# Where split operands begin in SBUF: four weight slots at offsets of 16 bytes, the rest on multiples of 128

## The chip, the cores and the metric

The kernel runs on one core of one Trainium2 chip. The metric is the device time of one execution in microseconds; the kernel before takes 3706.04 us (median of 3 runs, 3702.63 to 3710.48).

## What is computed

The reference is a trunk of two layers over 512 frames of width 1024, in float32. A layer is:

```python
x = layer_norm(ALPHA * x + 0.5 * swiglu(x, ffn_w12[l, 0], ffn_w3[l, 0]), ...)   # D_FF = 2816
x = layer_norm(ALPHA * x + hybrid_mixer(x, ...), ...)
x = layer_norm(ALPHA * x + memory_cross_attention(x, mem, wq, wkv, wo), ...)
x = layer_norm(ALPHA * x + 0.5 * swiglu(x, ffn_w12[l, 1], ffn_w3[l, 1]), ...)
...
def swiglu(x, w12, w3):
    g, u = jnp.split(x @ w12, 2, axis=-1)
    return (jax.nn.silu(g) * u) @ w3
```

The mixer is one input projection that feeds a gated DeltaNet (4 heads), an RG-LRU and a chunked band attention (8 heads), three gated branches added up, and an output projection. The cross attention has 4 heads over 256 memory tokens.

## The kernel before

**Split operands.** All large products are made of pairs: a float32 value is held as a high part rounded to float32r and a low part, the remainder, also float32r. `three` (L449) makes one product of a 128x128 block of weights and 512 columns with three matmuls: high weights by high data, high weights by low data, low weights by high data. Each has its own weight load. The pairs are wh/wl (weights), xh/xl (the layer's x), hh/hl (the inner values of the ffn), ych/ycl and yah/yal (branch outputs), mh/ml (merged branches), oh/ol (outputs of the cross attention), meh/mel (memory).

**The stream of weights.** All weights come from one array, in_stream, in 496 units of 128 x 1024 floats (512 KB): 248 for each layer, in the order of use. SyncE's queue loads unit u into slot u % 4 of raw (L414). GpSimd splits it: `split` (L429 on) writes wh[:, s, :] (L430, a multiply by one that rounds), and then wl[:, s, :] = raw - wh (L432). TensorE waits for the split (`unit_here`) and works through the unit's eight blocks of 128 columns, 24 matmuls where the moving operand has 512 columns; its first matmul of a unit (`unit_begun`) lets GpSimd write the slot of the unit before it.

**The stages of a layer**, in TensorE's program order, with the number of matmuls of `three` or of its like in one layer: ffn_up0 44 tiles of 24 = 1056; ffn_down0 8 tiles of 66 = 528 (22 blocks, three units a tile); att_qk 192; att_v 96, in which xh, xl are the stationary operand and the weights move; lru_x and lru_g 192, put in parts between the heads of the band attention; the mixer 1248 (proj 384 and gate 576 on x, up 288 on yah/ych), of which parts fill TensorE between the dependent steps of the four DeltaNet heads (`fill`); mix_out 192 on mh/ml; mem_k 192 with 256 columns on meh/mel; mem_v 96, with meh, mel as the stationary operand and the weights moving; x_q 192; x_out 192 on oh/ol; ffn_up1 and ffn_down1 as before. A bank of acc comes free when ScalarE or VectorE has read it. After each output projection comes a layer norm, in which TensorE waits.

**Where tensors begin.** The allocator places the tensors of trunk one behind the other in each partition, each at the next multiple of 32 bytes; xf begins at byte 16,512, a multiple of 128. Sizes for each partition: xf, xh, xl, raw, wh, wl 16,384 bytes each, const 5120, par 588, then tmp0 to tmp3, y_sum, sq_sum 2048 each, ones and mean_w 512 each, three eps tensors and warm of 4 bytes. What follows is shared by the stages in turn (`ExitStack`s): hh, hl; or ych, ycl, rows and what is of the mixer; or xq, oh, ol and what is of the cross attention. This gives, modulo 128:

| begins at, modulo 128 | before | with the change |
|---|---|---|
| xf, xh, xl, raw, const, par | 0 | 0 |
| wh, slots 0 to 3 | 0, 0, 0, 0 | 0, 16, 32, 48 |
| wl, slots 0 to 3 | 0, 0, 0, 0 | 64, 80, 96, 112 |
| tmp0 to tmp3, y_sum, sq_sum, ones, mean_w | 96 | 96 |
| hh, hl, ych, ycl, yah, yal, mh, ml, oh, ol, meh, mel | 96 | 0 |
| aq, ak, av, sc, pt, xq, xk, mraw, gate_w, decay, mt, qk, kg, kd, vk, dx, dz, dc, eg, state, vn | 96 | 0 |

Of the kernel before, what the change touches and what calls it, by code (L numbers as in the profile page):

```python
# [19 lines left out]
F32 = mybir.dt.float32  # L20
F32R = mybir.dt.float32r
ALU = mybir.AluOpType
# [3 lines left out]
P = 128  # L26
# [24 lines left out]
UNIT = 1024  # L51
SLOTS = 4
LEVELS = 7


PHASES = [("ffn_up0", 2 * KF, 2 * KF), ("ffn_down0", KD, 3 * KD), ("att_qk", 2 * KB, 2 * KB),
# [49 lines left out]
FILL = {"sum_k": 9, "k_turned": 3, "inv0_turned": 6, "rms_sums": 2}  # L106
FILL |= {f"p{s}": 2 for s in range(1, LEVELS)} | {f"qt{s}": 1 for s in range(1, LEVELS)}
FILL |= {"w": 1, "v1": 1, "v2": 1, "v3": 1}
# [37 lines left out]
C_ID, C_CAUSAL, C_FLIP, C_LEVEL = 0, P, 2 * P, 3 * P  # L146
CONST = (3 + LEVELS) * P

# [11 lines left out]
class StepSignal:  # L160
# [10 lines left out]
    def done(self, ins, step):  # L171

        assert self.steps[self.next % len(self.steps)] == step, (step, self.steps[self.next % len(self.steps)])
        self.next += 1
        return ins.then_inc(self.sem, 1)


class Chain:
# [12 lines left out]
    def loop(self, count, links):  # L191
        with self.eng.Fori(0, count) as i:
# [7 lines left out]
DN_PE = (["sum_k", "sum_q", "decay_rows", "k_turned", "v_turned", "a01", "a23", "inv0_turned"]  # L200
         + [f"{x}{s}" for s in range(1, LEVELS) for x in (("p", "qt", "q") if s < LEVELS - 1 else ("p", "qt"))]
         + ["w"] + [f"{x}{c}" for c in range(CH) for x in (("v", "o", "s") if c < CH - 1 else ("v", "o"))]
         + ["rms_sums"])
FILL_ORDER = DN_PE
DN_ACT = (["th1", "th0", "th2", "sq_k", "sq_q", "std_k", "std_q", "exp_g", "decay_exp", "kd_exp", "last_exp", "kg", "vk",
           "inv0"] + [f"p{s}" for s in range(1, LEVELS)] + ["w", "o", "o_sq", "rms_std", "z_th", "y_hi"])
DN_DVE = (["conv1", "conv0", "conv2", "silu1", "silu0", "silu2", "g_row", "k_normed", "q_normed",
           "g_last", "decay_min", "kd_arg", "decay", "kd", "m", "qk", "c0", "t0", "q_dec"]
          + [f"{x}{s}" for s in range(1, LEVELS) for x in (("c", "t", "n") if s < LEVELS - 1 else ("c", "t"))]
          + [f"{x}{c}" for c in range(CH) for x in (("v", "s") if c < CH - 1 else ("v",))]  # L210
# [18 lines left out]
def trunk(nc, xT, memT, stream, par_d, ba_w_d, gate_w_d, table_d, const_d, ext_d, outT):  # L229
    with ExitStack() as ctx:  # L230
        def sem(name):
            return ctx.enter_context(nc.semaphore(name))

        def sb(name, shape, dt=F32, scope=ctx):
            return scope.enter_context(nc.sbuf_tensor(name, shape, dt))
# [3 lines left out]
        xh = sb("xh", [P, KD, SEQ], F32R)  # L239
        xl = sb("xl", [P, KD, SEQ], F32R)  # L240
        raw = sb("raw", [P, SLOTS, UNIT])
        wh = sb("wh", [P, SLOTS, UNIT], F32R)
        wl = sb("wl", [P, SLOTS, UNIT], F32R)
        const = sb("const", [P, CONST])
        par = sb("par", [P, PAR])
        tmp = [sb(f"tmp{n}", [P, SEQ]) for n in range(4)]
# [4 lines left out]
        eps_rms = sb("eps_rms", [P, 1])  # L251
        eps_l2 = sb("eps_l2", [P, 1])
        eps_0 = sb("eps_0", [P, 1])
        warm = sb("warm", [P, 1])


        with ExitStack() as ffn:
# [80 lines left out]
        hi_step, unit_split, unit_begun = sem("hi_step"), sem("unit_split"), sem("unit_begun")  # L338
# [58 lines left out]
        def wait_apart(eng, sem_, value):  # L397

            eng.wait_ge(sem_, value)
            eng.sem_inc(waited_apart, 1)  # L400
# [4 lines left out]
        @block.sync  # L405
        def _(sp):
            sp.dma_start(xf[:, :, :], xT.rearrange("(k p) t -> p k t", p=P)).then_inc(x_loaded, 16)
            for s in range(SLOTS):
                sp.dma_start(raw[:, s, :], stream[s]).then_inc(unit_loaded[s], 16)

            with sp.Fori(1, ROUNDS) as i:
                for s in range(SLOTS):
                    sp.wait_ge(unit_split, i * SLOTS + (s - SLOTS + 1))
                    sp.dma_start(raw[:, s, :], stream[i * SLOTS + s]).then_inc(unit_loaded[s], 16)  # L414

            sp.wait_ge(x_hi.sem, x_hi.start + DEPTH * x_hi.per_layer)
            sp.dma_start(outT.rearrange("(k p) t -> p k t", p=P), xf[:, :, :]).then_inc(out_stored, 16)
            sp.wait_ge(out_stored, 16)

        @block.gpsimd  # L420
        def _(pool):
            pool.dma_start(const[:, :], const_d).then_inc(const_loaded, 16)
            pool.memset(ones[:, :], 1.0).then_inc(consts_set, 1)
            pool.memset(mean_w[:, :], 1.0 / DM).then_inc(consts_set, 1)
            pool.memset(eps_rms[:, :], NORM_EPS).then_inc(consts_set, 1)
            pool.memset(eps_l2[:, :], 4 * NORM_EPS).then_inc(consts_set, 1)
            pool.memset(eps_0[:, :], 0.0).then_inc(consts_set, 1)

            def split(i, s):  # L429
                pool.tensor_scalar(wh[:, s, :], raw[:, s, :], 1.0, 0.0, ALU.mult, ALU.add).then_inc(hi_step, 1)  # L430
                pool.wait_ge(hi_step, i * SLOTS + (s + 1))
                pool.tensor_tensor(wl[:, s, :], raw[:, s, :], wh[:, s, :].bitcast(F32), ALU.subtract).then_inc(unit_split, 1)  # L432

            for s in range(SLOTS):
                pool.wait_ge(unit_loaded[s], 16)
                split(0, s)
            with pool.Fori(1, ROUNDS) as i:
                for s in range(SLOTS):
                    pool.wait_ge(unit_loaded[s], i * 16 + 16)

                    wait_apart(pool, unit_begun, i * SLOTS + (s - SLOTS + 2))
                    split(i, s)

        @block.tensor
        def _(pe):
# [209 lines left out]
            def fill(l, parts, branch_a=False):  # L655

                for _ in range(parts):
                    if mixer_at[0] == len(mixer):
                        return
                    t, part = mixer[mixer_at[0]]  # L660
                    kind, a, b, u, at = MIXER[t]
                    if (kind, a) == ("up", 0) and not branch_a:
                        return
                    mixer_at[0] += 1
                    if part == 0:
                        if t < 4:
                            free_bank(l, "mixer", t - 3)
                        elif MIXER[t - 4][0] == "up":
                            pe.wait_ge(freed_d.sem, freed_d.at(l, FREE_D["mixer"] + MIXER_D[t - 4]))
                        else:  # L670
                            pe.wait_ge(freed_a.sem, freed_a.at(l, FREE_A["mixer"] + MIXER_A[t - 4]))
                        if at == 0:
                            unit_here(l, UNIT0["mixer"] + u)
                    o = acc[:, t % 4, :]
                    if (kind, a, b, part) == ("up", 1, 0, 0):
                        pe.wait_ge(lru_dve.sem, lru_dve.after(l, 0, "y_lo3"))
                    at += part * PART
                    k = (KB * a if kind == "up" else 0) + part * PART
                    last = unit(o, u % SLOTS, range(k, k + PART), at, of_y if kind == "up" else of_x, part == 0,
                                part == PARTS[t] - 1, begins=at == 0)  # L680
                    if part == PARTS[t] - 1:
                        last.then_inc(acc_ready.sem, 1)

            def delta(l):

                for h in range(HN):
# [45 lines left out]
                    done(last, "inv0_turned")  # L732
                    for s in range(1, LEVELS):
                        fill(l, FILL[f"p{s}"])
# [964 lines left out]
```

## Time and profile before

| | |
|---|---|
| median of 3 runs | 3706.04 us (3702.63 to 3710.48) |
| span of the profiled execution | 3702.0 us |
| TensorE matmuls busy | 3236.1 us, 87% |
| GpSimd, VectorE, ScalarE busy | 1757.6, 1690.1, 753.4 us |
| mean granted TensorE clock | 0.929 |

The profiled execution's own device time is not recorded beside its span; the span runs from its first to its last instruction, and is 4.0 us below the median of the runs. Matmuls are pipelined and their ends are modelled, so the time from the start of one to the start of the next (the pitch) says more than a duration.

### The profile page before, as it was taken

What the parts mean: (1) busy time and instruction counts of PE and PEld (TensorE: products, weight loads), DVE (VectorE), ACT (ScalarE), POOL (GpSimd) and SP (SyncE); (2) the same over time, 40 slices, a digit from 0 to 9 for tenths busy, and PEclk for the clock granted to TensorE, in tenths of its full rate; (3) what the DMA queues carried; (4) which work ended last, traced back from release to release, by engine and by line L of the source; (5) the groups of instructions that cost most, each with busy time, mean ns of one, the idle gap of its engine ahead of it and who ended that gap; (6) DMA issues with size and microseconds to landing.
All of it is one profiled execution on the core that took longest, in us unless ns stands there. A gap on an engine that the chain in (4) does not pass through costs nothing.

```text
span 3702.0 us, 41426 instructions
## 1 busy us (share of the span) xinstructions
PE 3236.1 (87%) x14024; PEld 2534.3 (68%) x14024; DVE 1690.1 (46%) x2034; ACT 753.4 (20%) x1305; POOL 1757.6 (47%) x1002
## 2 busy tenths in 40 slices
PE   7999899788869678999899998889888787889996
PEld 5888655666757555888678886557766565568884
DVE  3342555755436416333343325575555262263433
ACT  1110223222211222211021102342222112221101
POOL 5666433333306633666566664233332255246663
PEclk9999999899969888999999999999998798799998
DMA  3222211111102311222222222111111022113221
GB/s 129 96 97 102 87 52 48 55 52 52 52 18 85 104 56 51 96 96 97 91 86 96 97 102 83 35 57 57 52 52 46 29 91 91 40 63 107 96 97 51
DMA packets 78858, 272.53 MB, mean 74 GB/s; under 512 B 8176, under 2 KB 12560, under 8 KB 78736
## 3 DMA queue, kind: packets, MB, share of 16 engines
q1 hardware_dynamic: 73504, 264.27, 20.6%
q10 hardware_dynamic: 5088, 5.96, 0.5%
q8 instruction: 78, 1.28, 0.1%
q0 software_dynamic: 144, 0.66, 0.0%
q14 instruction: 44, 0.36, 0.0%
HBM read 268.73 MB, written 2.12 MB: 73 GB/s over the span
## 4 chain that ended last, share of the span: by engine, by line
PE 75%; DVE 12%; issue 7%; ACT 2%; POOL 2%; DMA 1%; DVEq 0%; POOLq 0%; ACTq 0%; SPq 0%
PE acc L447 65%; PE aux L447 9%; POOL wl L432 1%; DVE dc L1327 1%; POOL wh L430 1%; ACT tmp L886 1%; DVE dc L1325 1%; DVE tmp L1382 1%; DVE tmp L1525 1%; PE aux L592 1%; DVE tmp L1469 1%; DVE tmp L1472 1%; DVE xf L1251 1%; DVE xl L1200 0%; PE aux L834 0%
## 5 line engine op out<-in xcount | busy, mean ns | idle before, releaser
L430 POOL TENSOR_SCALAR wh<-raw 128x1024 fp32r<-128x1024 f32 x496 | 532.1, 1073 | 1849.9 <-PE acc L447 935.4
L432 POOL TENSOR_TENSOR wl<-raw,wh 128x1024 fp32r<-128x1024 f32 x496 | 1226.2, 2472 | 41.3
L447 PE MATMUL acc<-xh,wh 128*128 128x512 f32 x2432 | 989.8, 407 | 114.2 <-DVE xl L1200 57.4
L447 PE MATMUL acc<-xh,wl 128*128 128x512 f32 x2432 | 965.2, 397 | 0.0
L447 PE MATMUL acc<-xl,wh 128*128 128x512 f32 x2432 | 964.8, 397 | 0.0
L447 PEld LDWEIGHTS acc<-xh,wh 128*128 128x128 f32 x2432 | 467.3, 192 | 259.5 <-issue 101.4
L447 PEld LDWEIGHTS acc<-xh,wl 128*128 128x128 f32 x2432 | 466.9, 192 | 100.8
L447 PEld LDWEIGHTS acc<-xl,wh 128*128 128x128 f32 x2432 | 467.8, 192 | 94.3 <-issue 2.9
L447 PE MATMUL acc<-hh,wh 128*128 128x512 f32 x704 | 278.4, 396 | 0.0
L447 PE MATMUL acc<-hl,wh 128*128 128x512 f32 x704 | 278.4, 396 | 0.0
L447 PE MATMUL acc<-hh,wl 128*128 128x512 f32 x704 | 278.4, 396 | 0.0
L1200 DVE TENSOR_TENSOR hl<-tmp,hh 128x512 f32 x88 | 229.5, 2608 | 81.9 <-ACT hh L886 81.9
L1228 DVE SCALAR_TENSOR_TENSOR xf<-acc,xf 128x512 f32 x64 | 44.3, 692 | 364.7 <-PE acc L447 364.3
L1211 DVE TENSOR_TENSOR tmp<-tmp,acc 128x512 f32<-128x512 f32 x88 | 60.5, 688 | 275.3 <-PE acc L447 273.9
L1208 DVE SCALAR_TENSOR_TENSOR tmp<-tmp,acc 128x512 f32<-128x512 f32 x88 | 60.5, 687 | 247.2 <-ACT tmp L886 247.2
L886 ACT ACTIVATE tmp<-xf 128x512 f32 x64 | 40.5, 633 | 639.0 <-DVE xf L1228 639.0
L886 ACT ACT_TABLE_LOAD x93 | 119.3, 1283 | 229.5 <-PE acc L447 218.9
L1234 DVE TENSOR_TENSOR sq_sum<-sq_sum,tmp 128x512 f32<-128x512 f32 x64 | 159.3, 2490 | 2.2 <-ACT tmp L886 1.7
L447 PEld LDWEIGHTS acc<-hh,wh 128*128 128x128 f32 x704 | 132.2, 188 | 32.1
L447 PEld LDWEIGHTS acc<-hl,wh 128*128 128x128 f32 x704 | 132.2, 188 | 32.0
L447 PEld LDWEIGHTS acc<-hh,wl 128*128 128x128 f32 x704 | 132.2, 188 | 31.9
L1510 DVE TENSOR_TENSOR decay<-decay,aux 128x512 f32<-128x512 f32 x48 | 33.0, 688 | 244.9 <-PE aux L447 244.9
(257 smaller groups left out, 4002.5 us busy)
## 6 DMA issues: line engine op xcount, KB each, us to landing
raw<-in_stream SPq DMA_DIRECT2D x496, 512.0 KB, 3.2
xf<-in_xT SPq DMA_DIRECT2D x1, 2048.0 KB, 10.1
bias<-rel_scratch ACTq DMA_DIRECT2D x2, 1024.0 KB, 5.8
mraw<-in_memT ACTq DMA_DIRECT2D x2, 1024.0 KB, 5.2
out_xT<-xf SPq DMA_DIRECT2D x1, 2048.0 KB, 7.0
gate_w<-in_gate_w ACTq DMA_DIRECT2D x2, 512.0 KB, 3.3
const<-in_const POOLq DMA_DIRECT2D x1, 640.0 KB, 8.0
sc<-in_ba_w ACTq DMA_DIRECT2D x2, 256.0 KB, 2.6
```

The source lines that it names most:

```text
L430: pool.tensor_scalar(wh[:, s, :], raw[:, s, :], 1.0, 0.0, ALU.mult, ALU.add).then_inc(hi_step, 1)
L432: pool.tensor_tensor(wl[:, s, :], raw[:, s, :], wh[:, s, :].bitcast(F32), ALU.subtract).then_inc(unit_split, 1)
L447: return pe.matmul(out, w, x, start=start, stop=stop, skip_group_check=True)
L592: last = pe.transpose(aux[:, 2 + n % 2, j * P:(j + 1) * P], sc[:, i, j * P:(j + 1) * P], ident)
L886: return act.activation(out, in_, func, **kw)
L1200: return tt_(dst, whole, high.bitcast(F32), ALU.subtract)
L1208: stt_(tmp[1][:, :], tmp[0][:, :], 1.0, acc[:, 2 * m, :], ALU.add, ALU.mult).then_inc(freed_d.sem, 1)
L1211: tt_(tmp[2][:, :], tmp[1][:, :], acc[:, 2 * m + 1, :], ALU.mult).then_inc(freed_d.sem, 1)
L1228: stt_(xf[:, d, :], acc[:, n, :], factor, xf[:, d, :], ALU.mult, ALU.add).then_inc(freed_d.sem, 1)
L1234: tt_(sq_sum[:, :], sq_sum[:, :], tmp[3][:, :], ALU.add).then_inc(sq_added.sem, 1)
L1251: link(tt_(xf[:, d, :], xf[:, d, :], tmp[0][:, :], ALU.mult))
L1325: return ts_(dst, src, weight(3), None, ALU.mult)
```

## The change

In each of wh and wl a slot's row grows from 1024 to 1028 elements, so that each slot begins 16 bytes further on than a whole row of 4096 bytes; GpSimd writes and reads the first 1024 of them. The unused tensor warm (4 bytes) gives way to one of 64 bytes, line_fill, which nothing reads or writes either; it only moves what is allocated after it. TensorE's code is unchanged, since its blocks lie within the first 1024 elements.

```diff
+LINE = 32
+SKEW = 4
...
-        wh = sb("wh", [P, SLOTS, UNIT], F32R)
-        wl = sb("wl", [P, SLOTS, UNIT], F32R)
+        wh = sb("wh", [P, SLOTS, UNIT + SKEW], F32R)
+        wl = sb("wl", [P, SLOTS, UNIT + SKEW], F32R)
...
-        warm = sb("warm", [P, 1])
+        sb("line_fill", [P, LINE // 4 * 2])
...
-                pool.tensor_scalar(wh[:, s, :], raw[:, s, :], 1.0, 0.0, ALU.mult, ALU.add).then_inc(hi_step, 1)
+                pool.tensor_scalar(wh[:, s, 0:UNIT], raw[:, s, :], 1.0, 0.0, ALU.mult, ALU.add).then_inc(hi_step, 1)
                 pool.wait_ge(hi_step, i * SLOTS + (s + 1))
-                pool.tensor_tensor(wl[:, s, :], raw[:, s, :], wh[:, s, :].bitcast(F32), ALU.subtract).then_inc(unit_split, 1)
+                pool.tensor_tensor(wl[:, s, 0:UNIT], raw[:, s, :], wh[:, s, 0:UNIT].bitcast(F32), ALU.subtract).then_inc(unit_split, 1)
```

## Rows read from the trace of the kernel before

**Rows 1.** The page: busy time, share of the span and instructions of each engine.
```profile
PE 3236.1 (87%) x14024; PEld 2534.3 (68%) x14024; DVE 1690.1 (46%) x2034; ACT 753.4 (20%) x1305; POOL 1757.6 (47%) x1002
```
**Rows 2.** The page: the chain that ended last, by engine and by line.
```profile
PE 75%; DVE 12%; issue 7%; ACT 2%; POOL 2%; DMA 1%; DVEq 0%; POOLq 0%; ACTq 0%; SPq 0%
PE acc L447 65%; PE aux L447 9%; POOL wl L432 1%; DVE dc L1327 1%; POOL wh L430 1%; ACT tmp L886 1%; DVE dc L1325 1%; DVE tmp L1382 1%; DVE tmp L1525 1%; PE aux L592 1%; DVE tmp L1469 1%; DVE tmp L1472 1%; DVE xf L1251 1%; DVE xl L1200 0%; PE aux L834 0%
```
**Rows 3.** Timeline, ffn_up0: start us, us, engine line op out<-moving,stationary.
```profile
100.14 0.39 PE L447 MATMUL acc<-xh,wl 128*128 128x512 f32 x1
...
103.54 0.39 PE L447 MATMUL acc<-xh,wl 128*128 128x512 f32 x1
```
**Rows 4.** Timeline, ffn_down0.
```profile
300.20 0.40 PE L447 MATMUL acc<-hh,wl 128*128 128x512 f32 x1
...
309.30 0.40 PE L447 MATMUL acc<-hh,wl 128*128 128x512 f32 x1
```
**Rows 5.** Timeline, att_v of layer 0.
```profile
471.67 0.39 PE L447 MATMUL acc<-wh,xh 128*128 128x512 f32 x1
...
477.79 0.39 PE L447 MATMUL acc<-wh,xh 128*128 128x512 f32 x1
```
**Rows 6.** Timeline, mem_v of layer 0.
```profile
1268.52 0.39 PE L447 MATMUL acc<-wh,mel 128*128 128x512 f32 x1
...
1274.82 0.39 PE L447 MATMUL acc<-wh,mel 128*128 128x512 f32 x1
```
**Rows 7.** Groups of instructions: xcount | busy us, mean ns | idle before us.
```profile
L447 PE MATMUL acc<-hh,wh 128*128 128x512 f32 x704 | 278.4, 396 | 0.0
...
L447 PE MATMUL acc<-wh,meh 128*128 128x512 f32 x64 | 25.5, 398 | 1.1 <-ACT xk L886 1.1
...
L447 PE MATMUL acc<-wh,xh 128*128 128x512 f32 x64 | 25.1, 393 | 1.5 <-ACT ak L886 1.5
```
**Rows 8.** Timeline after a layer norm, and the stretch: busy (x), clock, DMA, GB/s.
```profile
412.50 0.63 PE L447 MATMUL acc<-xh,wl 128*128 128x512 f32 x1
...
413.78 0.63 PE L447 MATMUL acc<-xh,wl 128*128 128x512 f32 x1
...
411.50:414.00 2.50, 2.50 (x6) 2.02 (x7) 2.46 (x4) 1.75 (x3) 1.46 (x2) 0.50 0.00 0
```
**Rows 9.** Stretches: us, busy (x) of PE, PEld, DVE, ACT, POOL, granted clock, DMA, GB/s.
```profile
272.00:394.00 122.00, 122.00 (x525) 98.21 (x523) 34.94 (x25) 5.07 (x8) 84.19 (x48) 1.00 0.30 103
...
496.00:680.00 184.00, 157.75 (x580) 99.16 (x580) 120.86 (x217) 68.05 (x149) 53.28 (x30) 0.93 0.14 46
680.00:1160.40 480.40, 401.94 (x1940) 325.82 (x1939) 238.59 (x319) 105.44 (x172) 162.23 (x90) 0.88 0.14 49
...
1291.00:1348.00 57.00, 48.57 (x190) 38.38 (x191) 0.00 (x0) 4.43 (x8) 33.62 (x20) 0.88 0.27 92
1467.00:1711.00 244.00, 240.90 (x1056) 198.70 (x1056) 99.73 (x83) 49.20 (x67) 152.66 (x88) 0.99 0.27 93
```
**Rows 10.** Who TensorE waited for: us in total, times, longest us.
```profile
PE aux L447 <- ACT tmp L886: 76.5, 30, 9.8
...
PE acc L447 <- POOL wl L432: 52.3, 21, 16.0
```
**Rows 11.** One line's instructions, GpSimd and VectorE: duration ns min/median/max.
```profile
L430 POOL TENSOR_SCALAR wh<-raw x496: 1040/1052/1606, 12.2 to 3646.3; 128x1024 fp32r<-128x1024 f32 x166
...
L432 POOL TENSOR_TENSOR wl<-raw,wh x496: 2338/2395/2868, 13.3 to 3647.5; 128x1024 fp32r<-128x1024 f32 x166
...
L1327 DVE SCALAR_TENSOR_TENSOR dc<-dx,par,dc x72: 748/750/2769, 672.9 to 2830.2; 128x511 f32<-128x511 f32 x24, 128x510 f32<-128x510 f32 x24, 128x509 f32<-128x509 f32 x24
...
L1465 DVE SCALAR_TENSOR_TENSOR dc<-tmp,dc x24: 676/684/1519, 686.0 to 2832.1; 128x512 f32<-128x512 f32 x24
```
**Rows 12.** The same for TensorE's fp32 matmuls of a head.
```profile
L706 PE MATMUL aux<-const,dc x32: 270/272/328, 698.6 to 2844.3; 128*128 128x128 f32 x32
...
L447 PE MATMUL aux<-decay,tmp x384: 270/275/583, 721.0 to 2898.7; 128*128 128x128 f32 x192
```

## The prediction

> **What bounds the kernel now.** I read the page's share of each engine first: TensorE is busy 87% of the span, GpSimd 47%, VectorE 46% [rows 1]. The chain that ended last says the same by time: 75% of it is TensorE, and 65% is one kind of work, the matmuls into acc at L447, the streams of split operands; the splits on GpSimd (L432, L430) are 1% each [rows 2]. So what one matmul of those streams costs, start to start, sets most of the time, and a change of operand addresses must be judged there.
>
> The timeline gives that pitch. In the first up projection the moving operand (xh, xl) and the stationary one (wh, wl) both begin at a multiple of 128 bytes: the matmul that starts at 100.14 and the one 15 later at 103.54 give 3.40 / 15 = 226.7 ns [rows 3]. In the down projection the moving operands hh and hl begin at 96 past a multiple of 128: from 300.20 to 309.30 there are 39 matmuls, 233.3 ns [rows 4]. The 6.7 ns are no accident of the stage: the same pair appears where the roles are exchanged. In att_v the weights move and the stationary operand is xh (at 0): 471.67 to 477.79, 27 matmuls, 226.7 ns [rows 5]. In mem_v the code has the same form with meh, at 96, as stationary operand and the weights, at 0, moving: 1268.52 to 1274.82, 27 matmuls, 233.3 ns [rows 6]. The modelled durations agree: 393 ns on average for wh,xh and 398 for wh,meh, 396 for hh,wh [rows 7]. That decides the case: **a stationary operand that begins off the line slows the stream as much as a moving one does**, with the other operand at 0. In cycles of 2.4 GHz the two pitches are 544 and 560: one step of 16 elements, 64 bytes, more; 96 is 32 past a multiple of 64. At the granted clock of 0.50 the aligned stream has a pitch of 427 ns (412.50 to 413.78, three matmuls), which is 512 columns at 1.2 GHz and nothing over [rows 8]; there I expect no effect.
>
> **What the change does to addresses.** wh keeps its begin; its row grows by 4 elements per slot, so slots begin at 0, 16, 32, 48 past a multiple of 128, and every 512-byte block of weights in a slot has its slot's offset. wh is 64 bytes longer, so wl's slots begin at 64, 80, 96, 112. Together the two are 128 bytes longer, so what follows keeps its place within 128 until line_fill, whose 64 bytes bring hh, hl and the mixer's and the cross attention's split operands from 96 to 0. No instruction is added or removed, none moves between engines, and no wait changes. The price is all in the pitch.
>
> **Part 1, the moving operands come to 0.** By itself it takes 6.7 ns off each matmul that now has 233.3: down projections 4 x 8 tiles x 22 x 3 = 2112, mix_out 2 x 192 and x_out 2 x 192, together 2880; mem_v 192; the up tiles of the mixer 2 x 288 = 576. In ffn_down TensorE is busy 122.0 of 122.0 us [rows 9], so all of it would be on the path: 2880 x 6.7 = 19.2 us.
>
> **Part 2, the skew of the weights.** One unit in four (slot 0) stays on a multiple of 64, three are off. Which value for an offset? For 32 (slot 2: wh at 32, wl at 96) the row is mem_v's: 6.7 ns. For 16 and 48 no row shows a matmul; the bounds are 0 (only 32 matters) and 13.3 ns (twice the step seen), and I take 6.7, because a block of 512 bytes covers one 64-byte piece more from any begin that isn't on one, and one piece is just the 16 cycles seen. So a stream whose moving operand is at 0 costs on average 3/4 x 6.7 = 5.0 ns more than 226.7.
>
> **The sum.** Streams that are all at 0 now: ffn_up 4 x 44 tiles x 24 = 4224, att_qk 384, att_v 192, x_q 384, together 5184 matmuls; TensorE is busy 240.9 of 244.0 us in such an up projection [rows 9]. 5184 x 5.0 = +25.9; after each layer norm the clock is low for some matmuls and in x_q longer (0.88 over its window [rows 9]), for which I take 0.9 off: +25.0. Streams that pay 6.7 now and will pay 5.0: 2880 x 1.7 = -4.8, mem_v 192 x 1.7 = -0.3. mem_k has 256 columns and no aligned row to compare with; both parts touch its 384 matmuls in opposite ways, and I take 0. The mixer: 1920 matmuls on xh, +9.6, and 576 up, -1.0; but these fill TensorE while VectorE and ScalarE work on a head, which waits after them 76.5 us in all for ScalarE's tmp alone, and TensorE is busy 402 of 480 us there at a clock of 0.88 [rows 9, 10]. A longer fill shortens a wait where there is one. I take half of 8.6: +4.3, bounds 0 and 8.6. The 384 matmuls of lru_x and lru_g lie in the attention in the same way (158 of 184 us busy [rows 9]): +1.9, I take 1.0. The fp32 matmuls of a head whose moving operand (decay) comes from 96 to 0: median 275 ns now, against 272 for const at 0 [rows 12]; some 500 x 3 = -1.5.
>
> **GpSimd.** It now writes, and reads back, at 16, 32, 48. Its two instructions take 1052 and 2395 ns in the median [rows 11], 3.45 us a unit, where TensorE needs 24 x 226.7 = 5.44 us for one. That slack of 2.0 us hides anything likely. The nearest row on offsets is VectorE's: the convolution, which writes 4, 8 or 12 bytes past the begin of dc, has a median of 750 ns, the same operation on the whole of dc 684 [rows 11], 10%. Ten per cent on GpSimd is 0.35 us a unit, and TensorE waits for it 21 times, 52.3 us [rows 10]: at most 7 us. 16-byte steps are coarser than 4-byte ones; I take 0 and keep 0 to 7. VectorE and ScalarE at 0 instead of 96 show nothing: 0. Slower units would also hold VectorE's two-input instructions longer, hidden in the same slack.
>
> Sum: 25.0 - 4.8 - 0.3 + 4.3 + 1.0 - 1.5 = **+23.7 us**. The profiled span is 3702.0 and the median of the runs 3706.04, 4.0 above; the sum is a difference and goes on the median: **3730 us**, 0.64% slower. What a measurement of this kernel can tell from no change is about 0.2%, 7.4 us: 3698.6 to 3713.4.
>
> **A rule that speaks against this.** The trace shows that 96, a multiple of 16 and of 32, costs 6.7 ns, and that the stationary operand's begin matters to the matmul [rows 5, 6]. The Trainium skill (SBUF — State Buffer, Specifications) says that SBUF has cachelines of 16 bytes, and (TensorE: Matmul & The Clock Gate, Step-by-step: what each phase is for) that loading weights takes no read bandwidth from a running matmul, each having its own port. By these every slot would begin a cacheline, the skew would be free, and the time that of rival A; by the rows it isn't. The trace contradicts the second rule in mem_v, so I give it less than the rows.
>
> **Rivals.** A, **the skew is free and only part 1 counts**: what decides between the operands is then their begin relative to a cacheline smaller than 64 bytes, or mem_v is slow for another reason. Time: -19.2 (2880), -1.3 (mem_v), half of 576 x 6.7 = -1.9 on the path: -22.4 and with decay -24, 3682 to 3684. It decides if a slot at 16 and at 32 runs at 226.7. For it: nothing but the rule and that 16 and 48 are unseen. Against: rows 6. B, **only the offset of 32 costs**, 16 and 48 don't: 5184 x 1.7 = +8.6, 2880 x -5.0 = -14.4, mem_v -1.0, mixer and lru near +0.5, decay -1.5: -8, 3698, on the edge of no change. C, **16 and 48 cost twice**, 13.3: average (13.3 + 6.7 + 13.3) / 4 = 8.3. 5184 x 8.3 = +43, 2880 x 1.7 = +4.8, mixer and lru half of 16 and 3 = +9, decay -1.5: +55, 3761. D, **it is the distance between the two operands**, and a skew takes apart two reads that now collide: 96 against 0 is worse than 0 against 0 in either role, but 16 or 48 could be better. The floor is 512 columns at 2.4 GHz, 213.3 ns. With slots 1 and 3 at the floor and slot 2 at 233.3 the average is 221.7: 5184 x -5 = -26, 2880 x -11.7 = -34, the rest near -6: 3640.
>
> **How the numbers follow.** Forecast 0.55, A 0.17, B 0.11, C 0.11, D 0.06. The forecast's own range: the mixer's bounds (-4, +4), GpSimd's (0, +7), and wl's slot 0 at 64, which costs another quarter of a third of 6.7 ns, +4 on 8000 matmuls, if the line is 128 bytes: 3722 to 3746. For 8 times in 10 the range must take in A and B below, and most of C: 3682 to 3758. Faster by over 0.2% is A, D and nearly half of B: 0.27; within 0.2% the rest of B and a little of the forecast: 0.10; slower 0.63.
>
> **What would show it.** In the changed kernel's up projection the pitch should be 226.7 ns in one tile of four and 233.3 in three, so a pass of 1056 matmuls some 5 us longer; the down projection should have the same mix, 0.9 us shorter; mem_v's pitch should follow the slot now that meh is at 0. All tiles at 226.7 is A; only every fourth at 233.3 is B; 240 in two of four is C; anything under 226.7 is D. GpSimd's medians should stay at 1052 and 2395. I am wrong if a stationary block at 16 runs as fast as one at 0.

## The result and the profile after

The changed kernel takes 3730.13 us (median of 4 runs, 3724.02 to 3732.27) against 3708.26 us for the kernel before on the same chip: ratio 1.006, 95% interval 1.0043 to 1.0076, 22 us slower. The forecast was 3730. The sum held; the mechanism behind it held only in part, as one look at the pitch by slot shows. Ratios here and below are taken over the executions near each kernel's fastest; the one that this leaves out is an execution of e8 that took 11,824.56 us.

The page of the changed kernel, the rows that answer to [rows 1, 2]:

```profile
span 3726.2 us, 41426 instructions
PE 3259.3 (87%) x14024; PEld 2534.3 (68%) x14024; DVE 1696.3 (46%) x2034; ACT 753.8 (20%) x1305; POOL 1759.3 (47%) x1002
...
PE 76%; DVE 12%; issue 6%; ACT 2%; POOL 2%; DMA 1%; DVEq 0%; ACTq 0%; POOLq 0%; SPq 0%
```

The span is 24.2 us longer than before's 3702.0, and TensorE is busy 23.2 us longer; the busy time of each other engine is within 7 us of what it was. Nothing was added, so the instruction counts are the same. The next fence is the timeline of TensorE in the first up projection of the changed kernel, the first matmul of five units in a row (units 8 to 12, slots 0, 1, 2, 3, 0), 24 matmuls apart:

```profile
77.12 0.39 PE L450 MATMUL acc<-xh,wh 128*128 128x512 f32 x1
...
82.67 0.40 PE L450 MATMUL acc<-xh,wh 128*128 128x512 f32 x1
...
88.26 0.40 PE L450 MATMUL acc<-xh,wh 128*128 128x512 f32 x1
...
93.83 0.40 PE L450 MATMUL acc<-xh,wh 128*128 128x512 f32 x1
...
99.38 0.39 PE L450 MATMUL acc<-xh,wh 128*128 128x512 f32 x1
```

Slot 0 takes 5.55 us for 24, a pitch of 231.3 ns; slot 1 5.59 (232.9), slot 2 5.57 (232.1), slot 3 5.55 (231.3). Before, all four were at 226.7 [rows 3]. The mean over the projection is 231.9 ns, where I had 231.7, but slot 0 is not at 226.7 and no slot is at 233.3. In the down projection, before at 233.3 throughout [rows 4], the mean is 231.9 as well. The granted clock in both stages is 1.00:

```profile
277.50:399.70 122.20, 122.20 (x529) 98.96 (x527) 35.00 (x25) 5.07 (x8) 85.05 (x48) 1.00 0.31 103
1483.00:1727.00 244.00, 242.10 (x1045) 196.06 (x1044) 94.73 (x79) 47.72 (x64) 149.35 (x86) 1.00 0.29 93
```

(Stretches, columns as in [rows 9].) A down projection's stream takes 122.2 us where it took 123.0, and TensorE is busy 122.2 of 122.2.

Between the starts of the stages in the two timelines, the 24.2 us of the spans divide so (before, after, in us): the four up projections 255.7, 244.5, 248.0, 246.1 against 261.4, 249.9, 251.5, 251.4, +19.9; the down projections with their norms -4.1; the first half of att_qk with its product of ba_w, both layers, +2.7; the rest of attention +2.8; the mixer 487.8 and 482.3 against 486.8 and 484.7, +1.4; mix_out and its norm -1.8; x_q and the cross attention +3.7; the rest below half a microsecond. These are times of stages, with what the clock did in them: the third up projection of before had a granted clock of 0.98 where the changed kernel had 0.99, which makes that +3.5 smaller than the others. By pitch alone 4224 matmuls x 5.2 ns are 22.0 us.

GpSimd pays nothing for writing at 16, 32 and 48, against [rows 11]:

```profile
L435 POOL TENSOR_TENSOR wl<-raw,wh x496: 2340/2404/2892, 13.4 to 3673.2; 128x1024 fp32r<-128x1024 f32 x166
...
L433 POOL TENSOR_SCALAR wh<-raw x496: 1041/1050/1547, 12.2 to 3672.1; 128x1024 fp32r<-128x1024 f32 x166
```

Medians of 2404 and 1050 ns against 2395 and 1052.

### The profile page after: what moved, and what is told of

It is laid out like the page before. It is cut to its first block, busy times and chain, and to the rows that moved or that the text cites. A ratio compares the mean times of both kernels' runs of the same rounds, so it can differ in the third digit from the quotient of the medians.

```text
span 3726.2 us, 41426 instructions
## 1 busy us (share of the span) xinstructions
PE 3259.3 (87%) x14024; PEld 2534.3 (68%) x14024; DVE 1696.3 (46%) x2034; ACT 753.8 (20%) x1305; POOL 1759.3 (47%) x1002
## 4 chain that ended last, share of the span: by engine, by line
PE 76%; DVE 12%; issue 6%; ACT 2%; POOL 2%; DMA 1%; DVEq 0%; ACTq 0%; POOLq 0%; SPq 0%
PE acc L450 66%; PE aux L450 9%; DVE dc L1330 1%; POOL wl L435 1%; ACT tmp L889 1%; DVE dc L1328 1%; DVE tmp L1385 1%; DVE tmp L1528 1%; PE aux L595 1%; DVE tmp L1472 1%; DVE tmp L1475 1%; DVE xf L1254 1%; POOL wh L433 1%; DVE xl L1203 0%; PE aux L837 0%
## 5 line engine op out<-in xcount | busy, mean ns | idle before, releaser
L450 PE MATMUL acc<-xh,wh 128*128 128x512 f32 x2432 | 1001.6, 412 | 113.7 <-DVE xl L1203 57.4
L889 ACT ACT_TABLE_LOAD x93 | 119.3, 1283 | 232.8 <-PE acc L450 222.6
```

The lines of the kernel that those rows point to most:

```text
L450: return pe.matmul(out, w, x, start=start, stop=stop, skip_group_check=True)
L889: return act.activation(out, in_, func, **kw)
```

## The experiments

Two theories went in. **Pieces**, that of the prediction: each operand that is off a multiple of 64 bytes costs 16 cycles, wherever the other one begins. **Distance**: what counts is how far apart a matmul's moving and stationary operand begin, modulo some power of two; only the same place gives 226.7. Both fit all the rows of before, in which one operand was always at 0. A distance below is the begin of the moving operand minus that of the stationary one.

**e1_align_alone**, part one by itself:

```diff
-        warm = sb("warm", [P, 1])
+        sb("line_fill", [P, 16])
```

> The first part of the change alone: slots of the weights stay at 0 modulo 128, and line_fill brings hh, hl and the later split operands from 96 to 0. Both theories (pieces: each operand off a multiple of 64 bytes costs 16 cycles, wherever the other begins; distance: only two operands at the same place modulo 128 run at 226.7 ns, every other distance costs) expect 226.7 ns in every stream, the down projection 3.5 us shorter each, and 24 us less in all: 3684 us. A third theory, that the down projection is slow for its length or its banks and not for its begin, expects 233.3 ns there and 3706.

3695.65 us, ratio 0.9968 (0.9955 to 0.9982). Timeline, the first matmul of two units in a row, 24 matmuls apart, in the down projection and then in mix_out:

```profile
286.16 0.39 PE L447 MATMUL acc<-hh,wh 128*128 128x512 f32 x1
...
291.60 0.39 PE L447 MATMUL acc<-hh,wh 128*128 128x512 f32 x1
...
1177.88 0.39 PE L447 MATMUL acc<-mh,wh 128*128 128x512 f32 x1
...
1183.46 0.40 PE L447 MATMUL acc<-mh,wh 128*128 128x512 f32 x1
```

The pitch is as both theories expected, the time 12 us above their 3684 (see part one below). 5.44 / 24 = 226.7 ns: the down projection was slow for its begin, and each of the four streams is 119.5 us long instead of 123.0. But mix_out stays at 5.58 / 24 = 232.5 ns although mh begins at a multiple of 128. Modulo 256 xh, hh, oh and the weights are all at 128 here and mh is at 0: the first sign that 128 is not the period.

**e2_skew_alone**, part two by itself: the changed kernel with warm put back for line_fill.

> The second part alone: slots at 0, 16, 32, 48 (wh) and 64, 80, 96, 112 (wl), while hh, hl and the rest stay at 96. On x the pitch must be that of the changed kernel, 231.9 ns. In the down projection pieces expects the moving operand's 16 cycles and the weights' on top in three or four slots of four: about 239 ns, so 3742 us. Distance expects no sum of two costs: some 231 to 234 ns as before, 3732 to 3737 us.

3735.84 us, ratio 1.0082 (1.0065 to 1.0098). The down projection, from unit 4 (slot 0) to unit 5 and unit 6 to 7:

```profile
298.35 0.39 PE L450 MATMUL acc<-hh,wh 128*128 128x512 f32 x1
...
303.90 0.39 PE L450 MATMUL acc<-hh,wh 128*128 128x512 f32 x1
...
308.05 0.40 PE L450 MATMUL acc<-hh,wh 128*128 128x512 f32 x1
...
313.59 0.40 PE L450 MATMUL acc<-hh,wh 128*128 128x512 f32 x1
```

5.55 / 24 = 231.3 and 5.54 / 24 = 230.8 ns, and the mean of the projection is 230.7; on x it is 231.9, that of the changed kernel. With both operands off, the down stream is not at 239 but under the 233.3 that it has with one off. Costs of the two operands do not add: pieces falls here.

**e3_wl_at_64**, no skew at all, but 64 bytes behind wh and 64 behind wl, as the longer rows of the change put there:

```diff
+        sb("gap1", [P, 16])
         wl = sb("wl", [P, SLOTS, UNIT], F32R)
+        sb("gap2", [P, 16])
...
-        warm = sb("warm", [P, 1])
+        sb("line_fill", [P, 16])
```

> Part one plus 64 bytes between wh and wl, no skew: every slot has wh at 0 and wl at 64, as slot 0 of the changed kernel has, in which the pitch was 231.0 ns. Pieces of 64 bytes expects 226.7 ns (64 is a multiple of 64) and the time of part one alone, 3684 us; what slot 0 showed would then come from its neighbours. Distance modulo 128 expects 231 ns in every slot: 11,000 matmuls times 4.3 ns, of which some 9000 on the path, so 3684 + 39 = 3723 us.

3728.6 us, ratio 1.0058 (1.0041 to 1.0075). Up projection, units 8 and 9, then the down projection, two units in a row:

```profile
76.88 0.39 PE L449 MATMUL acc<-xh,wh 128*128 128x512 f32 x1
...
82.43 0.39 PE L449 MATMUL acc<-xh,wh 128*128 128x512 f32 x1
...
276.56 0.40 PE L449 MATMUL acc<-hh,wh 128*128 128x512 f32 x1
...
282.15 0.40 PE L449 MATMUL acc<-hh,wh 128*128 128x512 f32 x1
```

On x 5.55 / 24 = 231.3 ns, and the mean of every slot is 231.1. **This kernel has no skewed slot and costs as much as the whole change** (1.006). In the change, wl moved to 64 as a by-product of the longer wh; on x, that alone makes slot 0 slow.

But e3 differs from e1 in two things. The two gaps together are 128 bytes, so hh and oh, which e1 has at the place of the weights modulo 256, now begin 128 bytes off wh. The down projections are back at 233.3 ns and 123.0 us each, as before the change. Of the 33 us between e1 and e3, the profiles put 20 in the four up projections, where only wl moved, and 14 + 2.6 in the streams of the down projections and x_out. The changed kernel has the same 128 bytes: its line_fill brings hh and oh to 0 modulo 128, but not to the place of the weights modulo 256.

**e4_all_at_96**, everything off the line by the same distance: 24 floats ahead of xf.

```diff
+        sb("shift", [P, 24])
         xf = sb("xf", [P, KD, SEQ])
...
-        warm = sb("warm", [P, 1])
+        sb("line_fill", [P, 16])
```

> 24 floats ahead of xf: xf, xh, xl, raw, wh, wl at 96, and with the filler hh, hl and all later split operands at 96 too, so that all operands are off a multiple of 64 and at distance 0 from each other. Pieces expects 16 cycles for each of the two operands, 240 ns in every stream: 9000 x 13.3 over part one alone, about 3800 us. Distance expects 226.7 ns everywhere, 3684 us.

3693.98 us, ratio 0.9971 (0.9959 to 0.9984). Up projection, then down projection, a unit each:

```profile
76.05 0.39 PE L448 MATMUL acc<-xh,wh 128*128 128x512 f32 x1
...
81.49 0.39 PE L448 MATMUL acc<-xh,wh 128*128 128x512 f32 x1
...
292.29 0.39 PE L448 MATMUL acc<-hh,wh 128*128 128x512 f32 x1
...
297.73 0.39 PE L448 MATMUL acc<-hh,wh 128*128 128x512 f32 x1
```

5.44 / 24 = 226.7 ns in both, with every operand 32 bytes past a multiple of 64. (Only mix_out stays at 232.4, with mh 128 off modulo 256 as in e1.) The time is nearer to the 3684 us of distance than to the 3800 of pieces, and the pitch decides: **a line of 128 or 64 bytes has nothing to do with it; the distance has.**

The next four kernels come from one helper in `sb`, which puts an empty tensor ahead of each named one until it begins at a given place modulo 256:

```diff
+            at = -(-nc.sbuf_base // 32) * 32
+            gap = (BEGIN.get(name, at) - at) % 256
+            if gap:
+                scope.enter_context(nc.sbuf_tensor(f"gap_{name}", [P, gap // 4], F32))
             return scope.enter_context(nc.sbuf_tensor(name, shape, dt))
```

**e5_map_32**: `SKEW = 8`, wh and wl with the same place in slot 0 (128), xh, xl, oh, ol at 128, hh, hl, mh, ml at 0.

> A map of distances. Both wh and wl have slots that begin 0, 32, 64, 96 bytes further on; xh, xl, oh, ol begin where slot 0 does, hh, hl, mh, ml 128 bytes off (all modulo 256, since mix_out stayed at 232.4 ns in the kernel with part one alone, where mh is at 0 modulo 128 but 128 off modulo 256). If the pitch depends on the distance modulo 256: slot 0 has 226.7 ns on x and 232 on hh and mh; slots 1 to 3 on x (32, 64, 96) and on hh and mh (96, 64, 32) have 230 to 234 ns. If it depends on the distance modulo 128: slot 0 has 226.7 ns on hh too. If pieces of 64 bytes counted, slot 2 on x would have 226.7. Any pitch under 226.7 is news.

3733.35 us in one run (3701.92 before beside it). **e6_map_16**: `SKEW = 4`, wh, wl, xh, xl at 128, hh, hl at 0, mh, ml at 192, oh, ol at 64.

> The map in steps of 16: slots of both parts at 0, 16, 32, 48; xh, xl where slot 0 is, hh, hl 128 off, mh, ml 64 off, oh, ol 64 off the other way. Distance modulo 256 expects 226.7 ns in slot 0 on x alone and 230 to 234 ns in every other pair of slot and operand, 16 bytes no better than 32. If the lock tolerates a small distance, slot 1 on x (16 bytes) is at 226.7 as well.

3718.8 us in one run. Up projection of e6, units 8 to 11 and the next:

```profile
77.09 0.40 PE L453 MATMUL acc<-xh,wh 128*128 128x512 f32 x1
...
82.55 0.39 PE L453 MATMUL acc<-xh,wh 128*128 128x512 f32 x1
...
88.00 0.39 PE L453 MATMUL acc<-xh,wh 128*128 128x512 f32 x1
...
93.59 0.40 PE L453 MATMUL acc<-xh,wh 128*128 128x512 f32 x1
...
99.19 0.40 PE L453 MATMUL acc<-xh,wh 128*128 128x512 f32 x1
```

5.46 us, 5.45, 5.59, 5.60 for slots 0 to 3: 16 bytes are tolerated here, 32 and 48 are not. By the prediction's last sentence, that a stationary block at 16 which runs as fast as one at 0 would show it wrong, this is the sign. Slot by slot, the mean of all pitches under 250 ns in a stage, by the begin of the moving operand minus that of the weights (wh and wl alike), modulo 256:

| distance, bytes | pitch, ns | from |
|---|---|---|
| 0 | 226.7; 227.6, 228.6 | e1, e4 (x and hh); e6 and e5 x, slot 0 |
| -16; +16 | 227.0; 228.3 | e6 x slot 1; mh slot 3 |
| -32; +32 | 232.9 to 233.3; 233.2, 233.3 | before hh, e5 and e6 x; e6 mh, e5 hh |
| -48; +48 | 233.3; 232.6 and 231.8 | e6 x; mh of layers 0 and 1 |
| -64; +64 | 233.2, 233.4; 229.4, 229.8 | e6 oh, e5 x; e5 hh, e6 mh |
| -80; +80 | 231.7; 229.9 | e6 oh; hh |
| -96; +96 | 233.7, 234.0; 233.3 | e5 x, e6 oh; before mh, e6 hh |
| -112; +112 | 233.2; 231.1 | e6 oh; hh |
| 128 | 232.4 to 232.8 | e1 mh, e5 and e6 hh slot 0 |

Slot 0 of hh in e5, 128 off and so at distance 0 modulo 128, is at 232.8: the period is not 128. In e1 hh is 256 off the weights modulo 512, and at 226.7: a distance of 256 is harmless. Nothing lies under 226.7.

The prediction of e5 that slot 0 has 226.7 on x was missed: 228.6. In its units of slot 0 the first eight pitches average 231.4 ns, the following ones, up to the last, 226.7; in e6 the first four are at 232 and the rest at 226.7. Each such unit follows one of slot 3, 96 or 48 bytes off. So a matmul whose own operands are at the same place is slow for a while behind matmuls whose operands are not: the distance of its own pair isn't the whole condition.

All this is for 512 columns. **With 256 columns the sign turns.** mem_k (meh, mel moving) runs at 120.0 ns in e1, e4 and e8, where all its operands are at the same place modulo 256, at 118.3 before, where they are 32 apart, and at 115.9 in e3, where meh is 128 off wh. Two units in a row of e1, of before and of e3, 24 matmuls apart each (2.89, 2.84 and 2.77 us):

```profile
3048.22 0.28 PE L447 MATMUL acc<-meh,wh 128*128 128x256 f32 x1
...
3051.11 0.28 PE L447 MATMUL acc<-meh,wh 128*128 128x256 f32 x1
```

```profile
3052.71 0.28 PE L447 MATMUL acc<-meh,wh 128*128 128x256 f32 x1
...
3055.55 0.28 PE L447 MATMUL acc<-meh,wh 128*128 128x256 f32 x1
```

```profile
3077.72 0.27 PE L449 MATMUL acc<-meh,wh 128*128 128x256 f32 x1
...
3080.49 0.27 PE L449 MATMUL acc<-meh,wh 128*128 128x256 f32 x1
```

For this kernel it is little: 384 x 1.7 ns, 0.7 us, lost by the same place.

**e7_low_parts_64**: `SKEW = 0`; xl, wl, hl at 192 and their partners xh, wh, hh at 128; ol at 64.

> Which two reads meet? wl is 64 bytes off wh and xl, hl as far off xh, hh. While a matmul streams its moving operand the weights of the next one are loaded: xh beside wh, xl beside wl, xh beside wh. If the distance between those two reads counts, all three are at 0 here and x and hh run at 226.7 ns. If a matmul's own two operands count, xl,wh and xh,wl are 64 off, and the pitch is 231 ns or more. mh, ml (not moved) repeat the kernel with wl alone at 64: 231 ns. ol is 64 the other way, 128 from wl: 231 to 234 ns.

3722.38 us in one run. Up projection of layer 0, two units in a row, and the same in layer 1:

```profile
77.04 0.40 PE L453 MATMUL acc<-xh,wh 128*128 128x512 f32 x1
...
82.58 0.40 PE L453 MATMUL acc<-xh,wh 128*128 128x512 f32 x1
...
1906.12 0.39 PE L453 MATMUL acc<-xh,wh 128*128 128x512 f32 x1
...
1911.69 0.39 PE L453 MATMUL acc<-xh,wh 128*128 128x512 f32 x1
```

5.54 / 24 = 230.8 ns in the first; x and hh average 231.1 in every slot, except for the first ffn of layer 1, which has 232.2 up and down with the same begins (5.57 us for 24). mh repeats e3's 231.1, and ol's stream is at 233.3. The reads that I took to run at the same time are at distance 0 here, and it doesn't help. What remains is that a matmul's own two operands must be alike, or that the begins of successive moving ones must be, which this kernel changes too.

Neither reading is enough by itself. Counted for each of the three matmuls, from its start to the next one's, the means on x are 228.4, 229.2 and 235.8 ns in e3 (xh,wh; xl,wh; xh,wl) and 232.5, 231.7 and 229.2 in e7 (second up projections, both layers). The pair xh,wl is 64 bytes apart in both kernels, and it is the slowest of the three in one and the fastest in the other. In e3 all moving operands begin alike, and it is slow all the same.

**e8_all_mod_256** (`SKEW = 0`, all split operands at 128 modulo 256) and **e9_align_again** (the file of e1), in the same rounds:

> Part one made whole: wh, wl without skew, and all split operands at the same place as they modulo 256, yah, yal and mh, ml too, which part one alone leaves 128 off. Distance modulo 256 expects mix_out at 226.7 ns in place of 232.4 (384 matmuls, 2.2 us) and the mixer's product of yah the same (192 matmuls, up to 1.1 us): 2 to 3 us under part one alone, 3690 to 3693 us, and ratio 0.996 to the kernel before. If mix_out is slow for another reason (its place after the merge, ml's writes), it stays at 232.4 ns.

> Part one alone once more, in the same rounds as the kernel with yah and mh moved too: 0.9968 again, 0.0005 to 0.001 above the other, which these rounds can hardly tell.

e8: 3695.16 us, ratio 0.9969 (0.9957 to 0.9981). e9: 3691.16 us, ratio 0.9952 (0.9938 to 0.9967). e8 was expected at 3690 to 3693 us and below e9; it is above both, while e9 is below the 0.9968 expected. The intervals overlap, so moving yah and mh too gained nothing that can be told, although mix_out's pitch did what distance says, two units in a row of e8:

```profile
1182.76 0.39 PE L453 MATMUL acc<-mh,wh 128*128 128x512 f32 x1
...
1188.20 0.39 PE L453 MATMUL acc<-mh,wh 128*128 128x512 f32 x1
```

5.44 / 24 = 226.7. Where the 2.2 us of mix_out went is in its stretches (columns as in [rows 9]), of e1 first (both layers), then of e8:

```profile
1153.30:1200.00 46.70, 44.67 (x193) 35.86 (x191) 42.61 (x37) 5.08 (x8) 30.27 (x16) 1.00 0.26 89
2979.40:3026.10 46.70, 44.68 (x192) 35.90 (x191) 42.52 (x37) 5.08 (x8) 30.26 (x16) 1.00 0.26 88
```

```profile
1151.50:1198.80 47.30, 45.20 (x192) 36.91 (x192) 43.21 (x37) 5.07 (x8) 30.03 (x16) 0.96 0.27 88
2977.10:3024.40 47.30, 45.20 (x192) 36.95 (x191) 43.21 (x37) 5.07 (x8) 30.04 (x16) 0.96 0.26 88
```

The faster stream had a granted clock of 0.96 over the stage and took 47.3 us; the slower one had 1.00 and took 46.7. At 0.04 of 47.3 us, 1.9 us in each layer, the clock took back more than the pitch had won (1.1 us).

## Why the prediction was right, and where it wasn't

**The place of the cost: right.** No other engine's work changed, GpSimd's price is nil, and the up projections carry most: 4224 x 5.0 = 21.1 us predicted, 19.9 measured by stage. The down streams 4 x -0.8 = -3.2 measured, 2112 x -1.7 = -3.5 predicted. At the low clock nothing changed, as forecast: the pitches there have a median of 427 ns before and after.

**The unit of the price: wrong.** The step that failed is "a block of 512 bytes covers one 64-byte piece more from any begin that isn't on one", and with it that slot 0 stays fast, since wl's 64 is a multiple of 64, and that the others are at 233.3. Measured: 231.0, 233.2, 232.1, 231.2 for slots 0 to 3 on x. The prediction's two natural experiments [rows 4, 6] moved one operand against the other, by -32 and by +32 modulo 256, and I read them as a property of the operand. They were a property of the pair; no row of before had both at the same odd place, which e4 then supplied. The average came out right (231.9 against 231.7) because in the changed kernel no slot keeps distance 0 for both wh and wl, but all four cost less than 6.7 ns. Three slots of four at 6.7 and one at 0 is 5.0; the four measured, at 4.3, 6.5, 5.4 and 4.5, are 5.2. That is a coincidence of size and not a confirmation.

**Part one: the term too large, and not what the change does.** I had -24 us; e1 and e9 give ratios of 0.9968 and 0.9952, -12 and -18 us, with an interval of -7 to -23 between them. The down streams gave the 14 us forecast (4 x 3.5) and x_out 2 x 1.3. Missing are mix_out and the mixer's yah, 128 off, which is not the same place modulo 256: by pitch at most 4 us. Beyond that the forecast put a change of the clock at nothing. In e1's profile x_q with the cross attention of layer 0 takes 7.3 us more than before, at a lower granted clock, and the two stages of att_qk 4.1 us more; before first, both layers, then e1:

```profile
1291.40:1406.00 114.60, 89.51 (x320) 61.52 (x321) 17.71 (x55) 25.75 (x80) 33.22 (x20) 0.87 0.15 51
3113.70:3235.40 121.70, 96.59 (x321) 65.82 (x321) 17.93 (x55) 25.76 (x80) 33.26 (x20) 0.80 0.14 48
```

```profile
1282.70:1404.60 121.90, 96.41 (x320) 65.70 (x321) 17.85 (x55) 25.84 (x80) 33.69 (x20) 0.80 0.14 48
3108.90:3230.70 121.80, 96.35 (x319) 65.63 (x320) 17.84 (x55) 25.85 (x80) 33.59 (x20) 0.80 0.15 48
```

Either clock occurs with either layout, as before's second layer shows, so it is not shown to be an effect of the begins. But over whole executions the aligned kernels have the lower clock: 0.923 to 0.929 in those of e1 and e9, 0.926 to 0.931 in those of before beside them, 0.930 to 0.933 in those of the changed kernel. In the changed kernel itself part one was not done at all for the down projections: modulo 256 hh is 128 off wh there, which "what follows keeps its place within 128" hid. They run at 231.9 for that.

**Part two: too large as well.** Worked the prediction's way, part two is the difference of the sum and part one, +48 us; alone it measures 1.0082, +30 us. In the forecast the two misses cancel. The measured parts don't add up to the whole (-12 to -18 and +30, against +22), since with the longer wh and wl the filler no longer brings hh to the place of the weights. The forecast's own range was added up wrongly too: its terms give 3726 to 3745, not 3722 to 3746.

**The mixer** and the attention: +4.3 and +1.0 were taken, from half of the extra in the fills; the profiles show +1.4 and, with att_v in it, +2.8. But not for the reason given: the waits for ScalarE's tmp did not shrink, they went from 76.5 us [rows 10] to 79.7. TensorE's busy time in the stretch of the mixer stayed at 815 us, although each of its matmuls on x took 3.6 ns longer from start to start where the clock was full; the granted clock there rose a little. Both layers, before and then changed:

```profile
672.60:1160.40 487.80, 409.34 (x1960) 331.71 (x1961) 245.78 (x326) 106.07 (x173) 165.95 (x92) 0.88 0.14 49
2501.80:2984.10 482.30, 406.13 (x1961) 328.92 (x1962) 243.37 (x326) 106.28 (x173) 165.38 (x92) 0.89 0.14 50
```

```profile
682.40:1169.30 486.90, 411.10 (x1961) 330.83 (x1962) 246.47 (x326) 106.28 (x173) 165.17 (x92) 0.88 0.15 49
2521.00:3005.70 484.70, 404.15 (x1961) 326.89 (x1962) 245.34 (x326) 106.13 (x173) 164.66 (x92) 0.90 0.15 49
```

The term of the fp32 matmuls (-1.5) is not in the traces: the median of those with decay is 275 ns in both.

**The rivals.** A (skew free) is wrong for the change as made: part one alone runs at 3696 and the change at 3730. B and C go by offset of a slot and fail with slot 0. D named the right quantity, the distance between the operands, and the wrong sign: with 512 columns no distance is better than 0. With the 256 of mem_k its sign is right.

**The rules.** In the up projections e3 left the moving operand and wh where they were and moved wl by 64 bytes, and the stream's pitch rose from 226.7 to 231.1 ns. The Trainium skill (TensorE: Matmul & The Clock Gate, Step-by-step: what each phase is for) says that loading the next tile's weights doesn't take read bandwidth from the running matmul. No run here measures that bandwidth, and the sentence says nothing of addresses; what e3 shows is that with 512 columns the stationary operand's begin is not without effect on the stream. In the up projection of e6, 32 bytes of distance cost 6.3 ns a matmul and 16 bytes 0.3, both multiples of 16. The Trainium skill (SBUF — State Buffer, Specifications) gives SBUF cachelines of 16 bytes; the measurement goes beyond that, since every operand here begins on one.

## What to carry to other kernels

Where float32r matmuls, each with its own weight load, run back to back, compare the pitch of streams that differ only in where their operands begin: 226.7 against 233.3 ns is 3% of a stream, and one empty tensor of 64 bytes took it out (0.3 to 0.5% of this kernel). With 512 columns, give all operands of a stream the same begin modulo 256; with 256 columns that was the slowest place of those seen. Padding the rows of a buffer moves every tensor after it, so look up where those land: here the unnoticed 64 bytes under wl made the unskewed slot slow, and the 128 bytes of both kept hh off the place of the weights. Together they cost as much as the whole change, without any skew. And a natural experiment within a trace that varies one operand against a fixed other cannot tell a property of the operand from one of the pair.

## What the runs showed of the hardware

- The pitch of 128x128 by 512 float32r matmuls at a granted clock of 1.00, each with a weight load: 226.7 ns at distance 0 once the stream has settled, 227.0 and 228.3 at 16 bytes, 229 to 234 at other distances, not growing with the distance, with differences between + and - (233.4 at -64, 229.4 at +64).
- It also depends on what ran before: up to eight slow pitches behind a unit that is off (e5), and 231.1 or 232.2 ns with the same begins (e7).
- With 256 columns: 120.0 ns at distance 0 (e1, e4, e8), 118.3 at -32 (before), 115.9 in e3.
- At a granted clock of 0.50 the pitch with 512 columns is 427 ns (median) in the traces of all eleven kernels, whatever the begins.
- GpSimd's multiply and subtract of 1024 elements are as fast into begins at 16, 32 and 48 bytes as into multiples of 128 (1050 and 2404 ns against 1052 and 2395).
- Open: why 16 bytes are tolerated, why 64 costs less on one side, why 256 columns turn the sign, what in TensorE or SBUF waits. e7 leaves a matmul's own operands and the begins of successive moving ones, neither enough by itself; no run parts them.
